# Table loads on the sync queue, a later place for four stores, a second home for YP, and x's second quad turned inside the first weight tile

## The reference

```python
for i in range(2):
    h = rms_norm(x, norm_mix[i])
    x = x + (gmlp_mixer(h, ...) if i == 0 else s5_mixer(h, ...))
    x = x + (silu(h2 @ w1) * (h2 @ w3)) @ w2             # h2 = rms_norm(x, norm_ffn[i]), inner width 5632
    x = x + sigmoid(rms_norm(x, norm_ple[i]) @ w_gate) * (p[i] @ w_proj)
return rms_norm(x, norm_final)
# gmlp: z = gelu(h @ w_in); u, v = halves; (u * (tril(W_s) @ layer_norm(v) + b)) @ w_out
# s5:   u = h @ w_in; s_t = lam * s_(t-1) + B u_t per group (128 groups of 16 channels, 64 complex states)
#       y = Re(C s) + D u; g = gelu(y); halves of g @ w_out: val * sigmoid(gate)
```

## Time and profile before

| what | us |
|---|---|
| median of 3 runs | 2235.43 (2235.05 to 2237.21) |
| the profiled execution | 2235.3 |
| its span, first to last instruction | 2233.3 |
| TensorE busy | 2217.8 |
| VectorE, ScalarE, GpSimd busy | 1448.8, 1024.9, 493.1 |

### The profile page before, as it was taken

How to read it: one execution, slowest core, us unless ns; L and a number is a source line. 1 busy time by engine, 2 the same in 40 slices (tenths; PEclk the granted TensorE clock), 3 DMA queues, 4 the chain that set the end, 5 groups by cost and what they waited for, 6 DMA issues and landing times.

```text
span 2233.3 us, 28436 instructions
## 1 busy us (share of the span) xinstructions
PE 2217.8 (99%) x11280; PEld 1833.5 (82%) x11280; DVE 1448.8 (65%) x1612; ACT 1024.9 (46%) x1234; POOL 493.1 (22%) x470
## 2 busy tenths in 40 slices
PE   9999999999999999999999999999999999999998
PEld 7888888888888888888887788888888888888887
DVE  7879776667676666666668876555554445555666
ACT  5544444444434444445444454544444344444454
POOL 1246145456665544301003100000000000000001
PEclk9999999999999999999999999999999999999999
DMA  8668898988887898888789877777776667777774
GB/s 304 186 204 232 265 279 250 258 248 238 262 244 225 243 279 247 265 245 269 231 258 352 305 233 210 217 223 221 210 217 207 196 190 225 219 215 229 233 230 147
DMA packets 350677, 531.04 MB, mean 238 GB/s; under 512 B 106209, under 2 KB 127089, under 8 KB 349905
## 3 DMA queue, kind: packets, MB, share of 16 engines
q1 hardware_dynamic: 339456, 491.64, 73.5%
q0 software_dynamic: 8320, 30.75, 3.9%
q10 hardware_dynamic: 2768, 6.83, 0.9%
HBM read 475.67 MB, written 53.48 MB: 237 GB/s over the span
## 4 chain that ended last, share of the span: by engine, by line
PE 96%; DMA 1%; DVE 1%; issue 0%; ACT 0%; SPq 0%; ACTq 0%; DVEq 0%
PE PS L1636 62%; PE PS L1642 31%; DMA RAW<-in_s_w_out 1%; DMA X<-in_x 0%; DMA HT<-zd 0%; PE PS L1903 0%; PE PS L1904 0%; PE PS L1902 0%; PE PS L1740 0%; PE PS L1729 0%; DVE OP L1136 0%; PE PS L1667 0%; PE PS L1825 0%; DVE WLO L1110 0%; PE PS L1850 0%
## 5 line engine op out<-in xcount | busy, mean ns | idle before, releaser
L1636 PE MATMUL PS<-WHI,OP 128*128 128x512 f32 x6208 | 1537.8, 390 | 1.8 <-ACT YP L1023 1.4
L1110 DVE TENSOR_TENSOR WLO<-RAW,WHI 128x1024 fp32r<-128x1024 f32 x783 | 1020.5, 1317 | 687.8 <-ACT WHI L821 683.5
L1636 PEld LDWEIGHTS PS<-WHI,OP 128*128 128x128 f32 x6208 | 1162.3, 188 | 246.2 <-issue 3.6
L821 ACT ACTIVATE WHI<-RAW 128x1024 fp32r<-128x1024 f32 x783 | 827.5, 1062 | 999.6 <-PE PS L1642 644.7
L1642 PE MATMUL PS<-WLO,OP 128*128 128x512 f32 x3104 | 829.7, 389 | 1.3 <-DVE WLO L1110 1.3
L1642 PEld LDWEIGHTS PS<-WLO,OP 128*128 128x128 f32 x3104 | 582.5, 188 | 122.7 <-DVE WLO L1110 1.7
L805 POOL TENSOR_TENSOR ON<-X,GF 128x1024 f32<-128x1024 f32 x3 | 9.9, 3316 | 941.0 <-DVE X L1463 941.0
L706 POOL TENSOR_TENSOR TA<-BRAW,FAC 128x64 f32<-128x64 f32 x16 | 10.7, 669 | 267.4 <-DMA BRAW<-in_s_b_im 267.4
L869 ACT ACTIVATE S<-PS,RC 128x512 f32<-128x512 f32 x66 | 41.7, 684 | 37.0 <-PE PS L1642 36.9
L1136 DVE SCALAR_TENSOR_TENSOR OP<-HT,VEC,OP 128x128 fp32r<-128x128 f32 x120 | 38.2, 392 | 12.9 <-ACT OP L845 12.8
L1122 DVE TENSOR_TENSOR OP<-HT,OP 128x512 fp32r<-128x512 f32 x50 | 35.9, 760 | 15.4 <-ACT OP L836 15.4
(11 more groups left out here) (215 smaller groups left out, 956.6 us busy)
## 6 DMA issues: line engine op xcount, KB each, us to landing
RAW<-in_ffn_w SPq DMA_DIRECT2D x528, 512.0 KB, 4.3
RAW<-in_gm_w_in SPq DMA_DIRECT2D x64, 512.0 KB, 4.3
RAW<-in_s_w_out SPq DMA_DIRECT2D x64, 512.0 KB, 4.6
RAW<-in_ple_w_gate SPq DMA_DIRECT2D x56, 512.0 KB, 4.5
zd<-ZT SPq DMA_DIRECT2D x40, 512.0 KB, 3.2
HT<-zd SPq DMA_DIRECT2D x160, 128.0 KB, 5.0
RAW<-in_gm_w_out SPq DMA_DIRECT2D x32, 512.0 KB, 5.5
RAW<-in_s_w_in SPq DMA_DIRECT2D x32, 512.0 KB, 5.7
```

The source lines that it names most:

```text
L821: A_.activation(hi_of(t), raw_of(t), ACT.Copy).then_inc(hi_ready, 1)
L1110: V_.tensor_tensor(lo_of(t), raw_of(t), hi_of(t).bitcast(F32), ALU.subtract).then_inc(lo_ready, 1)
L1636: T_.matmul(dst[:, th, :], x_part, hi_of(t)[:, f], start=first and kk == 0 and part == 0, stop=False)
```

## The change

- In the first weight tile, turn(1) stands between the high and the low matmuls (a new argument of tile, between); turn(2) follows tile 1 and turn(3) tile 2.
- load_tq, load_td and load_tk move from GpSimd's list to the sync queue's, at the same tiles t, behind load t+6; the roots join that loop, and the waits for the last stores of the tables stand ahead of it. GpSimd keeps TE. TD_AT of duo 5 goes from 426 and 427 to 428 and 429.
- The stores of ROT stand behind loads 116, 120, 124, 128, not 104, 106, 108, 110; the memset of EXP[1] on GpSimd waits for split_used 108, not 102.
- YP has a second home, in Z's place, for duos 5 and 7 (Y_HOME); take_y waits for YG only of the last duo with the same home. At one tile take_y stands ahead of y_high, and y_high(4) comes one tile later (HIGH_AT).

```diff
--- before.py
+++ after.py
@@ -195,6 +195,8 @@
 OUT_BANK = [6] * (DUOS - 2) + [4, 4]
 Y_AT = [t + 2 for t in OUT_AT]
 DSET = [0, 1, 2, 0, 1, 0, 1, 0]
+Y_HOME = [0, 0, 0, 0, 0, 1, 0, 1]
+HIGH_AT = [t + (d == DUOS - 4) for d, t in enumerate(Y_AT)]
 
 G0 = start("gate0")
 TQ_AT = [(G0 + 1, G0 + 3), (G0 + 13, G0 + 15)]
@@ -202,7 +204,7 @@
 TK_AT = [(G0 + 9, G0 + 11), (G0 + 22, G0 + 24), (W0 + 4, W0 + 6)]
 TE_AT = [G0 + 12, G0 + 26]
 TQ_AT += [(W0 + g, W0 + g + 1) for g in (17, 20, 25, 28, 33, 35)]
-TD_AT += [(W0 + g, W0 + g + 1) for g in (22, 26, 30, 37, 39)]
+TD_AT += [(W0 + g, W0 + g + 1) for g in (22, 26, 32, 37, 39)]
 TK_AT += [(W0 + g, W0 + g + 1) for g in (24, 30, 32, 39, 41)]
 TE_AT += [W0 + g for g in (20, 23, 28, 31, 36, 38)]
 
@@ -355,7 +357,7 @@
         UT = place("UT", [P, 2, NW // 32, NC], at=pt_at)
         UP = [op_view(f"UP{i}", [P, 2, QB, QP, NC], 24 + 4 * i) for i in range(2)]
 
-        YP = place("YP", [P, 2, T, 2, CH], at=s_at)
+        YP = [place(f"YP{i}", [P, 2, T, 2, CH], at=(s_at, z_at)[i]) for i in range(2)]
         YG = place("YG", [P, 2, T, NC], at=s_at + 2 * KBYTE)
         VAL = f_view("VAL", [P, 2, NW], 0)
 
@@ -592,7 +594,7 @@
             loads_to(start("out0") + 12)
             load_b(0)
             for i in range(4):
-                loads_to(start("up0a") + 8 + 2 * i)
+                loads_to(start("up0a") + 20 + 4 * i)
                 if i == 0:
                     sp.wait_ge(rot_ready, 1)
                 ri, half = i // 2, i % 2
@@ -618,14 +620,46 @@
                         sp.dma_start(tabk[o], EXP[o % 2][:, :, :, :].rearrange("p j c i -> p (j c i)")).then_inc(k_out, 16)
 
 
-            for i in range(4):
-                loads_to(W0 + 6 + i)
+            def load_tq(d, bl):
+                if d >= 2:
+                    sp.wait_ge(in_done, d - 1)
+                sp.dma_start(TQ[d % 2][:, bl, :, :, :].rearrange("p q r n -> p (q r n)"), tabq[2 * d + bl]).then_inc(tq_in[d % 2], 16)
+
+            def load_td(d, bl):
+                if set_before(d) is not None:
+                    sp.wait_ge(out_of, set_before(d) + 1)
+                sp.dma_start(TD[DSET[d]][:, bl, :, :, :].rearrange("p q r n -> p (q r n)"), tabd[2 * d + bl]).then_inc(td_in[DSET[d]], 16)
+
+            def load_tk(d, bl):
+                sp.dma_start(TKK[DSET[d]][:, bl, :, :], tabk[2 * d + bl].rearrange("(g c) (j n) -> (c j) g n", g=GB, j=T)).then_inc(td_in[DSET[d]], 16)
+
+            def roots(i):
                 if i == 0:
                     sp.wait_ge(root_ready, RMS["win"] + 1)
                 for h in range(2):
                     for a in range(2):
                         sp.dma_start(ROOTU[32 * i + 16 * a:32 * i + 16 * a + 16, h:h + 1],
                                      ROOT[4 * h + i:P:8, a:a + 1]).then_inc(root_in, 16)
+
+            loads_to(G0 + RAWS - 1)
+            sp.wait_ge(q_out, 64 * KB)
+            sp.wait_ge(d_out, 16 * KB)
+            sp.wait_ge(k_out, 16 * KB)
+            for t in range(G0, TK_AT[DUOS - 1][1] + 1):
+                loads_to(t + RAWS - 1)
+                if W0 <= t < W0 + 4:
+                    roots(t - W0)
+                if t == G0:
+                    sp.wait_ge(split_used, t)
+                for d in range(DUOS):
+                    for bl in range(2):
+                        if t == TQ_AT[d][bl]:
+                            load_tq(d, bl)
+                        if t == TD_AT[d][bl]:
+                            load_td(d, bl)
+                        if t == TK_AT[d][bl]:
+                            load_tk(d, bl)
+
 
             loads_to(start("up1a") + 4)
             sp.dma_start(PN[:, :, :], p[1, 0].rearrange("(h p) d -> p h d", p=P)).then_inc(p1_in, 16)
@@ -733,7 +767,7 @@
                                  HALF[:, :].unsqueeze(1).unsqueeze(3).to_broadcast([P, 2 * QP, 2, CH]), ALU.mult)
                 if b == 0:
                     pool.wait_ge(ct_ready, 64)
-                    pool.wait_ge(split_used, start("up0a") + 6)
+                    pool.wait_ge(split_used, start("up0a") + 12)
                     step(G_.memset(EXP[1][:, :, :, :], 0.0))
                 c = lambda ri: CT[:, :, ri, b, :].unsqueeze(3).to_broadcast(shape)
                 up = lambda ri: LAMA[:, ri, pairs, :].unsqueeze(2).to_broadcast(shape)
@@ -759,19 +793,6 @@
                 decay(d)
 
 
-            def load_tq(d, bl):
-                if d >= 2:
-                    pool.wait_ge(in_done, d - 1)
-                pool.dma_start(TQ[d % 2][:, bl, :, :, :].rearrange("p q r n -> p (q r n)"), tabq[2 * d + bl]).then_inc(tq_in[d % 2], 16)
-
-            def load_td(d, bl):
-                if set_before(d) is not None:
-                    pool.wait_ge(out_of, set_before(d) + 1)
-                pool.dma_start(TD[DSET[d]][:, bl, :, :, :].rearrange("p q r n -> p (q r n)"), tabd[2 * d + bl]).then_inc(td_in[DSET[d]], 16)
-
-            def load_tk(d, bl):
-                pool.dma_start(TKK[DSET[d]][:, bl, :, :], tabk[2 * d + bl].rearrange("(g c) (j n) -> (c j) g n", g=GB, j=T)).then_inc(td_in[DSET[d]], 16)
-
             def load_te(d):
                 if d >= 2:
                     pool.wait_ge(rt_used, d - 1)
@@ -780,20 +801,10 @@
                 pool.dma_start(TE[d % 2][:, :, :, :].rearrange("p r q k -> p r (q k)"),
                                tabe.rearrange("r p n -> p r n")[:, :, DP * NC * d:DP * NC * (d + 1)]).then_inc(te_in[d % 2], 16)
 
-            pool.wait_ge(q_out, 64 * KB)
-            pool.wait_ge(d_out, 16 * KB)
-            pool.wait_ge(k_out, 16 * KB)
             pool.wait_ge(rot_out, 16 * 4)
-            for t in range(G0, TK_AT[DUOS - 1][1] + 1):
+            for t in range(G0, TE_AT[DUOS - 1] + 1):
                 pool.wait_ge(split_used, t)
                 for d in range(DUOS):
-                    for bl in range(2):
-                        if t == TQ_AT[d][bl]:
-                            load_tq(d, bl)
-                        if t == TD_AT[d][bl]:
-                            load_td(d, bl)
-                        if t == TK_AT[d][bl]:
-                            load_tk(d, bl)
                     if t == TE_AT[d]:
                         load_te(d)
 
@@ -1017,10 +1028,13 @@
 
             def take_y(d):
                 act.wait_ge(out_of, d + 1)
-                if d:
-                    act.wait_ge(yg_ready, d)
+                if Y_HOME[d]:
+                    act.wait_ge(ut_ready, NT)
+                earlier = [e for e in range(d) if Y_HOME[e] == Y_HOME[d]]
+                if earlier:
+                    act.wait_ge(yg_ready, earlier[-1] + 1)
                 for g in range(2):
-                    last = A_.activation(YP[:, :, :, g, :].rearrange("p b i c -> p b c i"),
+                    last = A_.activation(YP[Y_HOME[d]][:, :, :, g, :].rearrange("p b i c -> p b c i"),
                                          PS[:, OUT_BANK[d] + g, 0:2 * P].rearrange("p (b c i) -> p b c i", b=2, i=T),
                                          ACT.Gelu_apprx_tanh)
                 last.then_inc(yp_ready, 1)
@@ -1042,10 +1056,11 @@
                     if W0 + g == U_AT[n] + 4:
                         spread_u(n)
                 for d in range(DUOS):
-                    if W0 + g == Y_AT[d]:
-                        y_high(d)
                     if W0 + g == OUT_AT[d] + 1:
                         take_y(d)
+                for d in range(DUOS):
+                    if W0 + g == HIGH_AT[d]:
+                        y_high(d)
                 if W0 + g == end("out1", 0):
                     act.wait_ge(in_done, DUOS)
                     take("out1", 0, lambda th: VAL[:, th, :], ACT.Copy, scaled=False)
@@ -1545,7 +1560,7 @@
                 if d:
                     dve.wait_ge(y_ready, d)
                 V_.transpose(YG[:, :, :, :].rearrange("p b i k -> p (b i k)"),
-                             YP[:, :, :, :, :].rearrange("p b i g c -> p (b i g c)")).then_inc(yg_ready, 1)
+                             YP[Y_HOME[d]][:, :, :, :, :].rearrange("p b i g c -> p (b i g c)")).then_inc(yg_ready, 1)
 
             def y_low(d):
                 dve.wait_ge(y_hi, d + 1)
@@ -1625,7 +1640,7 @@
         def _(pe):
             T_ = nc.tensor
 
-            def tile(t, dst, block_, first, last_one):
+            def tile(t, dst, block_, first, last_one, between=None):
 
                 pe.wait_ge(hi_ready, t + 1)
                 for kk in range(TK):
@@ -1634,6 +1649,8 @@
                         for th in range(2):
                             x_part = OP_of(block_ + kk)[:, TOK * part + P * th:TOK * part + P * th + P]
                             T_.matmul(dst[:, th, :], x_part, hi_of(t)[:, f], start=first and kk == 0 and part == 0, stop=False)
+                if between is not None:
+                    turn(between)
                 pe.wait_ge(lo_ready, t + 1)
                 for kk in range(TK):
                     f = slice(NW * kk, NW * kk + NW)
@@ -1765,7 +1782,7 @@
                         k = j - (gate and j > PROJ_AT)
```

(8 more changed lines are left out.)

## The result

The changed kernel takes **2253.91 us** (median of 5 runs, 2252.81 to 2255.70), the kernel before 2235.43 (5 runs, 2234.96 to 2237.21): a ratio of 1.0083, 95% interval 1.0069 to 1.0096. It is slower by 0.8%. The forecast was 2252.2 with a range of 2247 to 2260.

What follows compares the result with a forecast made beforehand. TensorE's matmuls bound the kernel, 2217.8 of 2233.3 us. 2235.3 + 17.7 (stall) + 1.7 (clock) - 1.4 (tile 107) - 0.1 (start) - 1.0 (YP) + 0 (tables) = 2252.2 us, range 2247 to 2260.

Steps and rivals of the forecast that it cites:

- The reading of the list: Sync queue: block 1's matrices (BRAW) are fetched behind load 128 and the fourth ROT store, issued at about 355.6 us.
- Issue to GpSimd's first instruction: From BRAW's issue to GpSimd's start: 3.8 us plus 1.5 for one store, so GpSimd starts at 360.9 (359.4 to 365.0).
- The block: GpSimd making block 1's tables while VectorE waits for it: 19.5 us (bounds 17 and 27.3).
- Rival 3: GpSimd as slow on block 1 as before, 27.3 us, the rest as forecast: 2260.0 us; chance 0.08.
- The stall: TensorE waits for block 1 (d_ready 2) before the block matmuls after tile 124, from 362.7 to 380.4: 17.7 us.
- The clock: After the stall TensorE does about 3.4 us of work at half pace: 1.7 us lost (bounds 0 and 3.4).
- Tile 107: TensorE's wait for WLO goes, as stores and GpSimd's products leave this stretch: -1.4 us (bounds -1.4 and 0).
- The start: turn(1) no longer waits for x ahead of tile 0, which still needs its WHI: -0.1 us (bounds -0.7 and +0.5).
- YP: Tile 436: the second home lets take_y(5) go ahead of y_high(4), cutting TensorE's wait: -1.0 us (bounds -1.5 and +3).
- The tables: Moving 48 table loads from GpSimd's queue to the sync queue changes nothing: 0 us (bounds -1 and +4).
- rival 2: The tables' single list starves the state stage, at tiles 403 to 409 or TK of duos 6 and 7: 2260; chance 0.10.
- Rivals 1 and 2: Rival 1: block 1 is ready before TensorE asks, so not slower, 2232.8 us, chance 0.04; rival 2 has its own line.

Runs made afterwards that it cites:

- Experiments 1 to 3: 1: changed kernel, ROT stores and memset back, 2235.34 us; 2: changed kernel, block 1's matrices before the stores, 2234.13; 3: kernel before, these matrices behind load 128, 2252.57.
- experiment 8: Kernel before with only EXP's memset at tile 108, 2233.37 us; unchanged and profiled again, 2235.10; with only YP's second home and later y_high(4), 2235.66.
- b_best: Kernel before with the memset at tile 108, table loads on the sync queue and duo 2's TD at tiles 407 and 409: 2234.46 us.
- a_braw_first: Changed kernel with block 1's matrices asked for behind load 111, ahead of the four late ROT stores: 2234.13 us.
- b_tables_sync: Kernel before with only the 48 table loads and the roots on the sync queue, duo 5's TD at 428 and 429: 2235.46 us.
- a_dose16: Changed kernel with the ROT stores behind loads 112, 116, 120 and 124 instead of 116 to 128: 2244.71 us.

## Why the prediction was right, point by point

- **The reading of the list: right.** BRAW was forecast at 355.6 and issued at 355.19, right behind load 128 and the fourth store. Experiments 1 to 3 show it from both sides: the stores late without BRAW cost nothing that the runs can tell, BRAW late without the stores costs as much as the change.
- **Issue to GpSimd's first instruction: right.** Forecast 5.3 us (355.6 to 360.9), measured 5.1. The bounds of 3.8 and 9.4 were far apart, and that the quiet case plus one store came out to 0.2 us is in part luck: the two other kernels with a store right ahead of BRAW took 6.0 and 6.4.
- **The block: right.** Forecast 19.5 us, measured 19.0. The reason given, that GpSimd speeds up because VectorE waits for it, is visible in the rows: VectorE idle for 15.2 us before L1497, and GpSimd's products slow only beside the three low parts. Rival 3 (27.3 us) is out; the slowest block behind a late BRAW was 20.9, in the kernel where VectorE still had work.
- **The stall: right, slightly large.** 17.7 forecast; 17.09 more than before's gap. d_ready 2 came at 379.4, not 380.4, and TensorE was there at 362.3, not 362.7.
- **The clock: right mechanism, small size.** 1.7 forecast from 3.4 us at half pace, an estimate above the 2.8 us of transposes at half pace that the earlier trace rows shows; 2.34 measured, as the stretch at 1.2 GHz lasted some 5 us. Over four stalls it was 1.7 to 2.3.
- **Tile 107: right.** -1.4 forecast, -1.56 measured, in all eight profiles that had the memset at 108. I had put it down to stores and products together; it is the products alone (experiment 8). With the memset at 102 the five other profiles differ from before's by -1.3 to +2.8 us there. The wait grows with the time at which GpSimd can start the memset, and in five of the six the profile names the landing of CT as what it waited for: 0, 1.0, 1.3, 1.7, 2.2 and 2.5 us with starts at 303.94, 305.72, 305.89, 306.38, 306.57 and 308.45.
- **The start: right that it gives nothing.** -0.1 forecast, -0.19 measured, but the number means little: by tile 4 the seven profiles with the new order stand between -0.19 and +3.04 us against before, the seven with the old one between -0.27 and +1.39. What decides is not a wait. The three late ones (+3.04, +1.50, +1.39) wait no longer at the start than the others; their first matmuls run at half pace for longer (last section). The reordering shows no gain over that.
- **YP: the number came, the reason was wrong.** -1.0 forecast, -1.67 measured with tile 437. I had read the wait of 1.4 us as the buffer's. The second home alone leaves 1.1 us, and the sync queue's tables alone take 1.5 away. The step that failed is to treat one wait of one execution as a fixed part of the kernel: in a second profile of the same kernel it was absent. I had named the condition ("whose weight 438 may come no sooner") and not given it its price.
- **The tables: the term of 0 was mis-sized.** The step that failed is "with no weight due in between". A weight's due time isn't its own matmul alone: behind WHI and WLO of 403 stood the operand's low part, which was due one tile earlier. It was in the place that rival 2 named (tiles 403 to 409), but cost 1.1 us and not 8, and no table came late. As a whole, from tile 400 to 780, the state stage and what follows took 0.05 to 0.55 us more than in before in the seven profiles with the tables on the sync queue other than b_best (1.2 more there), and 0.15 to 0.89 less in the five other profiles with GpSimd's tables. The move doesn't pay; that it costs some tenths of a microsecond is as much as these single profiles bear.
- **Rivals 1 and 2** are out: no satisfied wait at L1757, no wait for TK, TD or WHI anywhere.
- **Two slips that touch no result:** the low end's own terms give 2247.35, not 2247.5 (2252.2 less 2.5, 1.5 and 0.85), and block 2's start would by the forecast's numbers be 4.9 us later against TensorE, not 3 (380.4 - 357.5, less 18.0); it was 4.2.

The two terms that carry the result were forecast at 19.4 us together and measured at 19.43: one 0.6 us too large, the other 0.6 too small, so the closeness of the sum is luck, its size is not. The rest, -2.5 forecast, was -1.7.

## What to carry over

When something is moved later in an in-order list, look first at what stands behind it, not at the thing itself: here four stores that nobody waits for took the input of a 19 us chain with them, and the fix is to ask for that input before them. Due times hold for everything that is queued behind a transfer's consumer on the same engine, not just for the consumer. And a wait of about a microsecond in one profile is worth a second profile of the same kernel before a change is built on it: of the three that this change was to cure, the one for YP was gone in the second profile, and the one for WLO was anything from 0 to 2.5 us in the six kernels that had done nothing about it.

## What the runs showed of the hardware that I had not expected

- VectorE's short two-input instructions suffer more from GpSimd than the reverse: eight of them took 7.55 us beside GpSimd's products and 2.19 alone, 3.4 times as long, while the five products that GpSimd began beside them took 1.07 to 1.30 us, hardly longer than alone (1.06 to 1.26). Beside VectorE's long low parts (128x1024) both lose: a product takes 1.93 to 2.12 us, a low part 1.93 on average instead of 1.22.
- What TensorE's restart at 1.2 GHz costs didn't grow with the pause: 1.69, 1.97, 2.34 and 1.69 us after 8.8, 15.3, 17.0 and 26.4 us.
- The first microseconds differ by up to 3 us between executions, and the pace of TensorE's matmuls is why, not its waits. Tile 1 starts between 11.53 and 15.10 in the 14 profiles. In the three latest, tile 0's high matmuls start one every 0.43 us at first, and one every 0.23 in all the others. TensorE's timelines of a_braw_first, b_tables_sync and the changed kernel:

```profile
8.56 3.75 PE L1653 MATMUL PS<-WHI,OP 128*128 128x512 f32 x8 [1.18 <-DVE OP L1163]
```

```profile
9.61 3.17 PE L1645 MATMUL PS<-WHI,OP 128*128 128x512 f32 x8
```

```profile
8.17 2.09 PE L1651 MATMUL PS<-WHI,OP 128*128 128x512 f32 x8 [1.59 <-DVE OP L1161]
```

The granted clock from 2.4 to 16 us reads 1.00 in every profile, so at the start it doesn't show the half pace; the durations do. Kernels with the very same instructions up to there fall on both sides (the changed kernel and a_dose16 differ by 1.7 us at tile 4). Why the half pace lasts longer in some executions stays open. The medians of the kernel before still agree to 0.02% (2235.15 to 2235.53 in four groups of runs).
